# Delta rule: output with tokens on partitions, inverse transposed in blocks on VectorE

## What is computed

```python
def l2_normalize(x, eps=1e-6):
    return x * rsqrt(sum(x * x, axis=-1, keepdims=True) + eps)

def gated_delta_rule(q, k, v, g, beta):        # chunks of C tokens, state (Dk, Dv) per head
    q = q * Dk ** -0.5
    g = cumsum(g)                              # inside a chunk
    decay = where(causal, exp(g_i - g_j), 0)
    k_beta = k * beta
    a_mat = where(strict, (k_beta @ k.T) * decay, 0)
    t_inv = inverse(eye + a_mat)               # unit lower triangular
    u = t_inv @ (v * beta)
    w = t_inv @ (k_beta * exp(g))
    qk = where(causal, (q @ k.T) * decay, 0)
    for each chunk i:
        v_new = u_i - w_i @ state
        o_i = (q_i * exp(g_i)) @ state + qk_i @ v_new
        state = state * exp(g_last) + (k_i * exp(g_last - g_i)).T @ v_new

o_c = gated_delta_rule(l2_normalize(q_c), l2_normalize(k_c), v_c, g, beta)
o_c = rms_norm(o_c, gnorm_w) * silu(z_c)
```

## Time and profile before

| | |
|---|---|
| median of 3 runs | 1328.27 us (1324.42 to 1328.39) |
| the profiled execution, own time | 1331.17 us |
| its span in the profile | 1329.4 us |
| TensorE busy | 1306.1 us, 98% of the span |
| VectorE / ScalarE busy | 653.1 us (49%) / 498.2 us (37%) |
| TensorE's share of the chain that ended last | 92% |
| first delta step to first gated product | 707.05 us to 919.80 us |

### The profile page before, as it was taken

One profiled execution on the slowest core, in us unless ns is written; L12 is line 12 of the kernel. 1 busy time (PEld: TensorE's weight loads), 2 busy tenths in 40 slices (PEclk: granted clock), 3 DMA queues, 4 the chain that ended last, 5 costly groups with the idle time before them and its releaser, 6 DMA issues.

```text
span 1329.4 us, 17079 instructions
## 1 busy us (share of the span) xinstructions
PE 1306.1 (98%) x6413; PEld 1060.1 (80%) x6413; DVE 653.1 (49%) x936; ACT 498.2 (37%) x731; POOL 13.9 (1%) x22
## 2 busy tenths in 40 slices
PE   9999989999999999999999999999999999999997
PEld 6776547888888878888888988888888888878886
DVE  6676766644444442228656436434544444442224
ACT  6343325533333331125554444444433333332111
POOL 0000000000000000000001010000000000000000
PEclk9999989999999999999989999999999999999998
DMA  6232220332222233322212101001322222223221
GB/s 238 90 100 81 76 70 33 100 116 99 96 95 95 95 97 102 101 95 67 94 62 80 48 17 48 33 33 42 117 95 95 95 95 95 95 95 111 95 79 64
DMA packets 34080, 114.02 MB, mean 86 GB/s; under 512 B 4466, under 2 KB 4722, under 8 KB 34034
## 3 DMA queue, kind: packets, MB, share of 16 engines
q1 hardware_dynamic: 33266, 112.29, 25.5%
q10 hardware_dynamic: 768, 1.09, 0.3%
HBM read 106.90 MB, written 2.10 MB: 82 GB/s over the span
## 4 chain that ended last, share of the span: by engine, by line
PE 92%; DVE 3%; ACT 3%; DMA 1%; issue 1%; ACTq 0%; SPq 0%; DVEq 0%
PE PS L1372 90%; DMA raw<-w_stream 1%; PE PS L1448 1%; PE PS L1784 1%; DVE wring L951 1%; ACT wring L560 1%; DVE hbuf L1220 0%; DVE outT L1366 0%; DMA reps<-ub 0%; ACTq L676 0%; ACT HH L564 0%; PE PS L1665 0%; ACT lnsq L688 0%; DVE amax L1016 0%; DVE lnsq L1114 0%
## 5 line engine op out<-in xcount | busy, mean ns | idle before, releaser
L1372 PE MATMUL PS<-HH,wring 128*128 128x512 f32 x3096 | 730.8, 394 | 0.0
L1372 PEld LDWEIGHTS PS<-HH,wring 128*128 128x128 f32 x3096 | 577.5, 189 | 120.7 <-issue 3.4
L1372 PE MATMUL PS<-AA,wring 128*128 (+1 forms) x1320 | 303.0, 390 | 1.7 <-DVE ubuf L922 1.6
L1372 PEld LDWEIGHTS PS<-AA,wring 128*128 128x128 f32 x1320 | 247.3, 188 | 54.4 <-DVE ubuf L922 2.4
L922 DVE TENSOR_TENSOR ubuf<-PS,rstd 128x512 f32<-128x512 f32 x44 | 30.4, 691 | 198.1 <-PE PS L1372 198.1
L944 DVE TENSOR_TENSOR wring<-raw,wring 128x1024 fp32r<-128x1024 f32 x36 | 44.1, 1226 | 149.6 <-ACT wring L611 149.6
L931 DVE TENSOR_TENSOR wring<-raw,wring 128x1024 fp32r<-128x1024 f32 x88 | 107.5, 1222 | 0.9 <-ACT wring L603 0.4
L951 DVE TENSOR_TENSOR wring<-raw,wring 128x1024 fp32r<-128x1024 f32 x70 | 85.3, 1221 | 42.6 <-ACT wring L560 42.6
L560 ACT ACTIVATE wring<-raw 128x1024 fp32r<-128x1024 f32 x70 | 73.6, 1055 | 79.2 <-PE PS L1372 57.2
L598 ACT ACTIVATE AA<-ubuf 128x512 f32 x44 | 27.9, 633 | 198.4 <-DVE ubuf L929 198.4
L611 ACT ACTIVATE wring<-raw 128x1024 fp32r<-128x1024 f32 x36 | 38.2, 1061 | 155.5 <-PE PS L1372 155.5
(11 more groups left out here) (252 smaller groups left out, 1028.2 us busy)
## 6 DMA issues: line engine op xcount, KB each, us to landing
raw<-w_stream SPq DMA_DIRECT2D x194, 512.0 KB, 3.3
reps<-ub SPq DMA_DIRECT2D x48, 66.5 KB, 2.1
out_t<-outT SPq DMA_DIRECT2D x8, 256.0 KB, 2.2
xT<-x_t SPq DMA_DIRECT2D x3, 512.0 KB, 8.8
reps<-ub ACTq DMA_DIRECT2D x16, 66.5 KB, 2.2
first_raw<-w_stream SPq DMA_DIRECT2D x2, 512.0 KB, 9.8
rope<-rope_const SPq DMA_DIRECT2D x1, 576.0 KB, 6.8
consts<-shape_const SPq DMA_DIRECT2D x1, 576.0 KB, 7.7
```

The lines of the kernel that those rows point to most:

```text
L1372: return nc.tensor.matmul(out, lhsT, rhs, start=start, stop=stop)
```

## The change

The block's chain of steps is rewritten, from 27 to 20 matmul steps, and the list's order with it.

- The transposes of `R` for levels 1 to 5 are done by VectorE, as one instruction over 128 x 512 that transposes each 32 x 32 square (`V.transpose(T, R)`, L1301 and L1312 after). Up to there `R` has nothing outside its 32 x 32 squares on the diagonal. The corner transpose of the last level stays on TensorE. `STEP_T0` and ScalarE's copies of `T` go.
- The query scale is not multiplied in any more; the norm's epsilon is multiplied by (sum of squares + 1e-6) x 128 instead (`qeps`), one small VectorE instruction earlier in the kernel. The `picked` product of step 1 and its VectorE product go.
- `w` is no longer made. VectorE multiplies `kbT` by the decay (into `kT`), `STEP_W` multiplies that by the state, VectorE subtracts the product from the values (`vd`, L1317), and `STEP_V` is one product with the inverse. GpSimd's `kbe` goes.
- Block 0 has no state to read: no `STEP_W`, half a `STEP_O`, a copy in place of decay and sum, no clearing of the state.
- `STEP_O` gives tokens on partitions (`qe.T @ state + qkT.T @ vn`). ScalarE squares it with four 128-column instructions that also sum the columns (`accum_out`); no products with ones. VectorE scales it by token (L1337) before `STEP_B`, which is now four transposes; ScalarE writes them to `qT` with the norm's weight.

```diff
-PE_STEPS, ACT_STEPS, DVE_STEPS, POOL_STEPS = 27, 19, 21, 3
+STEP_Z1, STEP_Z6, STEP_W, STEP_V, STEP_O, STEP_S, STEP_B, STEP_N = 2, 13, 15, 16, 17, 18, 19, 20
+def gdn_list(i):
+    return [k for k in list(range(STEP_S + 1)) + [STEP_N, STEP_B] if not (i == NB - 1 and k == STEP_S) and not (i == 0 and k == STEP_W)]
...
-PLAN = ("tktttktatbttattttbtatbtttatabtatbabatabtabtabtatbtabtabtabtatbeeooabeotbeeaoeoebooeeaobeoateebtoaeae"
+PLAN = ("ktttttkatbtatbtttttattattbtbttababttatabttatabtatbabatbattabeeooaeotaeebooteeooaeeooaeoaabteettootbeeab"
...
 # GpSimd
-        nc.gpsimd.memset(St_b, 0.0).then_inc(sem("state_zero"), 1)
-                    nc.gpsimd.tensor_tensor(gbufs[st][3], ktok[:, i], per_head(kscal[1][:, i]), ALU.mult).then_inc(gdn_pool[st], 1)
...
 # ScalarE
-            elif k == STEP_T0:
-                run(k, Tb, X)
-            elif k == STEP_W:
-                run(k, Tb, X, scale=-1.0)
...
             elif k == STEP_O:
-                run(k, qT[:, :, blk(i)], X)
-                nc.scalar.activation(qe, hd(X), ACT.Square).then_inc(gdn_act[st], 1)
+                product(k)
+                for h in range(H):
+                    ins = nc.scalar.activation(qe[:, h], PS[:, X, blk(h)], ACT.Square, accum_out=ost[:, 0, 4 * i + h:4 * i + h + 1])
+                ins.then_inc(made, 1)
+            elif k == STEP_B:
+                product(k)
+                nc.scalar.activation(qT[:, :, blk(i)], hd(Y), ACT.Copy, scale=vcol(V_GNORM)).then_inc(made, 1)
...
 # VectorE
-            V.tensor_scalar(qscal, l2s[:, :, 0:4], SC_FOX, None, ALU.mult)
-            V.tensor_tensor(kscal[1], kscal[0], gexp[:, 0], ALU.mult)
+                V.tensor_scalar(qeps, PS[:, 7, 0:32].rearrange("p (a b) -> p a b", b=8)[:, :, 0:4], 1e-6, 1e-6 * P, ALU.add, ALU.mult)
...
-                V.tensor_tensor(qT[:, :, blk(i)], qT[:, :, blk(i)], hd(X), ALU.mult).then_inc(mine, 1)
+                V.tensor_tensor(kT[:, :, blk(i)], kbT, eg, ALU.mult).then_inc(mine, 1)
...
+                made("R0")
+                V.transpose(T, R).then_inc(mine, 1)
...
+                if n < 5:
+                    made(f"R{n}")
+                    V.transpose(T, R).then_inc(mine, 1)
+            elif k == STEP_W:
+                V.tensor_tensor(vtok[:, i], vtok[:, i], hd(X), ALU.subtract).then_inc(mine, 1)
...
-                V.scalar_tensor_tensor(qT[:, :, blk(i)], qT[:, :, blk(i)], vcol(V_GNORM), hd(Y), ALU.mult, ALU.mult).then_inc(mine, 1)
+                V.tensor_tensor(qe, hd(X), per_head(ost[:, 1, some]), ALU.mult).then_inc(mine, 1)
...
 # TensorE
-                last = picked(PS[:, X], PICK_Q + i)
...
-                    dve_done(10 + n)
-                    for h in range(H):
-                        last = nc.tensor.transpose(PS[:, X, blk(h)], R[:, h], ident)
...
-                last = heads(X, lambda h: kbe[:, h], lambda h: R[:, h])
+                dve_made("state", i - 1)
+                last = heads(X, lambda h: kT[:, h, blk(i)], lambda h: St_b[:, h])
...
-                    mm(PS[:, Y, blk(h)], R[:, h], vtok[:, i, h], True, False)
-                    last = mm(PS[:, Y, blk(h)], wT[:, h], St_b[:, h], False, True)
+                last = heads(Y, lambda h: R[:, h], lambda h: vtok[:, i, h])
...
-                    last = token_sum(PS[:, X, h:h + 1], osq[:, h])
...
-                    last = spread(PS[:, Y, blk(h)], ost[:, 1, 4 * i + h:4 * i + h + 1])
+                    last = nc.tensor.transpose(PS[:, Y, blk(h)], qe[:, h], ident)
```

More of the change, by code:

```diff
@@ L89, in odd_tile, with gdn_made, gdn_count @@
     return T_IN1 + e + (1 if e >= HEAD_TILE else 0)
-PE_STEPS, ACT_STEPS, DVE_STEPS, POOL_STEPS = 27, 19, 21, 3
-STEP_T0, STEP_Z1, STEP_W, STEP_V, STEP_O, STEP_S, STEP_N, STEP_B = 3, 4, 21, 22, 23, 24, 25, 26
-STEP_Z6 = STEP_Z1 + 15
+STEP_Z1, STEP_Z6, STEP_W, STEP_V, STEP_O, STEP_S, STEP_B, STEP_N = 2, 13, 15, 16, 17, 18, 19, 20
+def gdn_list(i):
+    return [k for k in list(range(STEP_S + 1)) + [STEP_N, STEP_B] if not (i == NB - 1 and k == STEP_S) and not (i == 0 and k == STEP_W)]
+def gdn_made(engine, i):
+    levels = [x for n in range(1, 5) for x in (f"R{n}", f"T{n}")]
+    if engine == "pe":
+        return [k for k in gdn_list(i) if k != STEP_N]
+    if engine == "act":
+        return ["eg", "decay", "Z1", "Z2", "Z3", "Z4", "Z5", "T5", "Z6", "vn", "osq", "root", "normed"]
+    state = [] if i == NB - 1 else ["state"] if i == 0 else ["state_decayed", "state"]
+    return (["kbT", "gaps", "masked", "qe", "decay", "NT", "qkT", "kbeT", "eye", "R0", "T0"] + levels + ["R5", "R6"]
+            + (["vd"] if i else []) + state + ["ms", "rms", "scaled"])
+def gdn_count(engine, i, name):
+    return sum(len(gdn_made(engine, j)) for j in range(i % 2, i, 2)) + gdn_made(engine, i).index(name) + 1
 SLOTS = (("g", 0, 0), ("g", 0, 1), ("q", 2), ("q", 3), ("g", 1, 0), ("g", 1, 1), ("q", 4), ("q", 5), ("c", 0), ("g", 2, 0), ("g", 2, 1),
@@ L771, in gdn @@
         def gdn(i, k):
[L772 removed]
+            st = i % 2
             X, Y = 4 + 2 * st, 5 + 2 * st
             Zb, Tb, Rb, qe = gbufs[st][0], gbufs[st][1], gbufs[st][2], gbufs[st][5]
[L775 to L779 removed]
+            made = gdn_act[st]
@@ L1264, in gdn @@
                 product(1)
[L1265 to L1272 removed]
+                made("decay")
@@ new lines, in gdn @@
+            elif k == STEP_W:
+                dve_made("state", i - 1)
+                last = heads(X, lambda h: kT[:, h, blk(i)], lambda h: St_b[:, h])
+            elif k == STEP_V:
+                dve_made("R6")
+                if i:
+                    dve_made("vd")
+                else:
+                    pe.wait_ge(gdn_pool[st], gdn_pools(i)[0])
+                last = heads(Y, lambda h: R[:, h], lambda h: vtok[:, i, h])
+            elif k == STEP_O:
+                act_made("vn")
+                for h in range(H):
+                    if i:
+                        mm(PS[:, X, blk(h)], qe[:, h], St_b[:, h], True, False)
+                    last = mm(PS[:, X, blk(h)], qkT[:, h], vn[:, h], i == 0, True)
+            elif k == STEP_S:
+                pe.wait_ge(gdn_pool[st], gdn_pools(i)[1])
+                last = heads(Y, lambda h: ktok[:, i, h], lambda h: vn[:, h])
+            elif k == STEP_B:
+                dve_made("scaled")
+                for h in range(H):
+                    last = nc.tensor.transpose(PS[:, Y, blk(h)], qe[:, h], ident)
```

197 lines of the change are left out of this document (88 added, 109 removed).

## The result

| | before | after |
|---|---|---|
| median, in the same comparison | 1326.51 us (4 runs, 1324.42 to 1328.39) | 1302.85 us (4 runs, 1300.62 to 1304.17) |
| ratio | | 0.9822, interval 0.9807 to 0.9836 |
| span and granted clock of the profiled execution | 1329.4 us, 0.989 | 1302.1 us, 0.994 |
| delta stage, first `picked` to first `y_high` product | 707.1 to 919.8, 212.7 us | 701.3 to 893.8, 192.5 us |
| TensorE busy in it, and its waits | 211.4, 1.2 | 190.9, 1.5 |

The account below looks back on a forecast made before the run. TensorE was taken as the bound, busy 98% of the span. Work -20.1, new waits +1.3 and -0.3 ahead of the stage gave -19.1 us, from 1328.27 to 1309.2 us; range 1303 to 1317.

Parts of the forecast that it names:

- nothing outside moves by more than 1 us: Before 697 us and behind the first `y_high` product, no part of the kernel moves by more than 1 us.
- TensorE's work, -20.1 us: Delta stage, four blocks: removed transposes, state products, `spread`, sums and `picked` products, costed by their turns, save 20.1 us.
- The rival that costed by busy records (28 us): TensorE in the delta stage: removed instructions save their group's busy time, 28 us; gain 22 to 28, about 1303; chance 0.10.
- The transpose, 0.69 us, cost 0: VectorE in the delta stage: each of 20 block transposes takes 0.69 us, covered by TensorE's other work, costing 0.
- half eaten by queues: Delta stage: transposes cost 1.3 to 1.8 us or VectorE's queue runs late; gain 5 to 15, about 1318; chance 0.17.
- cover ends at x = 1.24: Delta stage: a block transpose is covered up to 1.24 us; without that cover, x - 1.24 at each place.
- a transpose of 3 us: Case of the rival that the kernel gets slower, block transposes far above every row: about 1343 us; chance 0.03.
- New waits, 2.5 instead of 1.2 us, +1.3: TensorE in the delta stage: the new order brings 2.5 us of waits in place of 1.2, adding 1.3 us.
- The three named places: TensorE waits at step 1 of block 0 (0.4 us), step 1 of block 2 (0.6), corner transpose of block 3 (1.0).
- others, small: 0.5: Delta stage: further small new waits of TensorE, beyond the places named, 0.5 us together.
- Ahead of the stage, -0.3: Before the delta stage TensorE waits 1.67 us for the scalars; two small instructions on that way go, 0.3 us less.
- The sum, -19.1: Whole kernel: -20.1 + 1.3 - 0.3 = -19.1 us, taken from the median 1328.27 to give 1309.2.

Follow-up runs that it names:

- e_vt: Kernel before, old order, with only the inverse's 80 TensorE transposes and ScalarE's copies replaced by 20 VectorE block transposes: 1320.50 us, ratio 0.9953.
- e_twice: Changed kernel with each of the 20 block transposes made twice: 1309.68 us, ratio 0.9873; stage 195.3 us.
- e_three: Changed kernel with each of the 20 block transposes made three times: 1323.73 us in one execution; stage 207.3 us.
- The later comparisons: Two repeats of the changed kernel, unedited, against the kernel before: 1306.46 us, ratio 0.9855, and 1306.50 us, ratio 0.9853.
- c_before: Kernel before, unedited, run again against itself: 1325.96 us against 1326.82, ratio 0.9998; stage 212.7 us.
- c_after: Changed kernel, unedited, run again against the kernel before: 1306.46 us, ratio 0.9855; stage 192.5 us.
- e_out: Kernel before, old order, with only the output turned to tokens on partitions and its summed squares on ScalarE: stage 210.5 us, one execution.

## Why the prediction came out as it did

The direction and the mechanism in the stage were right. The median is 0.15 us under the lower end of the range. The step that failed is the last one, from the stage to the median, with "nothing outside moves by more than 1 us"; one term of the sum, the waits, was also too large.

- **TensorE's work, -20.1 us.** Right: busy time in the stage fell by 20.5, and each part alone is within 1.1 us of its turns. The rival that costed by busy records (28 us) fell with it, although the first comparison's 23.7 us stands in its interval: the stage shows 20.2. (Its 28 also prices the 32 one-column passes as the others; by their own records it is 27.)
- **The transpose, 0.69 us, cost 0.** Right for this order, 0.711 and no wait behind one. In the old order it is not free: 2.4 us of `e_vt`'s waits stand behind transposes in VectorE's queue, which the prediction named only as the mechanism of its rival "half eaten by queues". That cover ends at x = 1.24 was too generous where that queue is not empty (`e_twice`, `e_three`). (By the prediction's own terms a transpose of 3 us would give 1344, not 1343.)
- **New waits, 2.5 instead of 1.2 us, +1.3.** Too large: 1.5 instead of 1.2. The three named places were right in place and nearly in size (0.23, 0.49, 0.82 for 0.4, 0.6, 1.0); the "others, small: 0.5" did not exist. The records on PE show each 0.2 to 0.4 short, and those of before 0.1 and 0.4.
- **Ahead of the stage, -0.3.** Right in kind: TensorE waits there 1.5 us for the pairs, had 1.67.
- **The sum, -19.1.** At equal clock 20.8 (20.2 in the stage, 0.2 ahead of it, the rest within what three digits of clock leave open). So 1.7 us were missed here, 1.0 of it by the waits and 0.4 by TensorE's work.
- **"Nothing outside moves by more than 1 us", and the step from the sum to the median.** This is the step that failed. Before's profiles alone differ by 8.9 us ahead of the stage, and 48 executions of it lie 10 us apart. I took 1328.27, the median of three, as a fixed point; the comparison's own was 1326.51, 1.8 us lower. And the medians of the first comparison differ by 2.9 us more than at equal clock: after's four executions were granted 0.993 to 0.996, above the mean of 0.992 (before's four are not on record, so this share is worked out, not read). 1.8 + 1.7 + 2.9 is the distance between 1309.2 and 1302.85. The later comparisons gave 1306.5 twice, inside the range, so that one comparison missed it and two would not have. The range was made of costs alone and held nothing for the clock, although the three runs shown, 1324.42 to 1328.39, and the profiled one, 1331.17, already lay 6.7 us apart.

The prediction did not weigh the arrangement as a term of its own. It counted waits along the new order, which was enough; but 8 of the 20 us would be gone with the old one.

Not tried: the stage with the block transposes on another engine, the new order in the kernel before, and a kernel that removes the 3.4 us wait ahead of the first fall of the clock, below.

## What to carry to other kernels

Where one engine is full, the work that a removed instruction takes from it is its turn in a full queue, not its record: the busy time of five parts confirmed it here within 1.1 us. How much of that the kernel gains is a matter of the order. Work that moves to a half empty engine still stands in that engine's queue, in front of results that others wait for, and a removed step can have been the distance between two others. So the parts, tried alone in the old order, showed 14.3 us and the whole in that order 11.9, against 20.2 in an order made for it. Compare stretches, or span times granted clock, before explaining a difference of a few us by the edit; give the range of a prediction room for the spread between executions; and keep the boundaries of a stretch at work that the edit does not reorder.

## What the runs showed of the hardware

The granted clock falls at the same few places of the kernel, but not in every execution. In the profile of before, TensorE waits 3.4 us for a DMA and then the clock is down from about 171 us on; in `c_before` the same wait lasts 3.2 us, and the clock stays at 1.00. The length of the wait does not decide it: `c_after` waits 3.1 us and its clock falls, `e_out` 3.3 us and its does not. The wait of before:

```profile
170.36 2.48 PE L1372 MATMUL PS<-reps,cw 128*32 128x512 f32 x12 [3.40 <-DMA reps<-ub]
```

At 676 us of before it falls without a visible wait ahead of it (busy 2.00 of 2.00 us in each stretch from 656 on):

```profile
674.00:676.00 2.00, 2.00 (x20) 2.00 (x19) 0.30 (x1) 2.00 (x5) 0.00 (x0) 0.97 0.00 0
676.00:678.00 2.00, 2.00 (x11) 2.00 (x11) 1.89 (x2) 0.66 (x2) 0.00 (x0) 0.50 0.04 8
```

A fall may also follow a new wait: in `e_three` TensorE waited 1.71 us from 732.6 and the clock then fell to 0.50, the lower level of 1.2 GHz, inside the stage, where it was at 1.00 in every other profile:

```profile
734.33 1.97 PE L1409 MATMUL PS<-G,G 128*128 128x128 f32 x8 [1.71 <-DVE G L1316]
...
733.00:735.00 2.00, 0.68 (x3) 0.68 (x4) 1.97 (x4) 0.25 (x1) 0.00 (x0) 0.87 0.00 0
735.00:737.00 2.00, 2.00 (x12) 2.00 (x11) 2.00 (x4) 0.60 (x1) 0.00 (x0) 0.50 0.00 0
737.00:739.00 2.00, 2.00 (x15) 1.96 (x15) 1.94 (x3) 0.00 (x0) 0.00 (x0) 0.78 0.00 0
```

One execution shows it, so that the wait was its cause is not shown. By the Trainium skill (TensorE: Matmul & The Clock Gate, "Part 1: The HAM clock gate") the clock is throttled by default and activity releases it. The falls at 171 and 734 agree, each behind a wait; the one at 676, behind twenty busy us, does not.
